# Moving the heads' norm, transposes and splits of two mixers among the units around them, on one core

## The reference, cut to what is computed

```python
def diff_attention(q, k, v, lam_vec, subln_g, lam_init):
    ...
    o = map_query_blocks(block, q)
    o = rmsnorm(o, subln_g) * (1.0 - lam_init)
    return o.reshape(B, S, A_W)
...
def odd_mixer(h, st_C, st_n, st_m, st_h, w_in, gate_b, conv_c, conv_d, conv_d_b,
              rg_wa, rg_ba, rg_wx, rg_bx, rg_lam, norm_g, w_out):
    ...
    hc = rmsnorm(hf + jnp.flip(hb, 2), norm_g)
    hc = hc.transpose(0, 2, 1, 3).reshape(B, S, C_W) * jax.nn.sigmoid(o)
    ...
    out = (jnp.concatenate([hc, hd], axis=-1) @ w_out).astype(h.dtype)
```

## Time and profile before

| | us |
|---|---|
| median of three runs | 1631.69 (1631.17 to 1632.00) |
| the profiled execution | 1632.15 |
| its span, first to last instruction | 1630.6 |
| PE, DVE, ACT busy in the span | 1477.7, 1050.4, 900.0 |
| experts, 923 to 1600 | 677.0 |

### The profile page before, as it was taken

The page is one execution under the profiler, slowest core; times in us unless marked ns, Lnnn a source line. Parts: engine busy times, 40 slices in busy tenths (PEclk is TensorE's granted clock), DMA queues, the critical chain, the costliest instruction groups (busy, mean ns, idle before and its releaser), DMA issues.

```text
span 1630.6 us, 19112 instructions
## 1 busy us (share of the span) xinstructions
PE 1477.7 (91%) x7385; PEld 1225.0 (75%) x7385; DVE 1050.4 (64%) x1270; ACT 900.0 (55%) x1062; POOL 93.2 (6%) x162
## 2 busy tenths in 40 slices
PE   4989798899999989997777899999999999999991
PEld 1987356699998878885456688888888888888881
DVE  2424546533233445894464798797987989879794
ACT  3422446533232445773155577677776877768773
POOL 0402500000000002000000200000000000000001
PEclk8999899999999999998898999999999999999996
DMA  9793990333342324224615799999999999999993
GB/s 361 206 392 119 322 338 22 103 104 104 125 134 103 129 72 161 104 80 157 238 55 207 286 351 391 371 399 374 390 389 359 408 376 392 391 367 403 379 377 129
DMA packets 146621, 414.52 MB, mean 254 GB/s; under 512 B 6924, under 2 KB 30888, under 8 KB 146408
## 3 DMA queue, kind: packets, MB, share of 16 engines
q1 hardware_dynamic: 134192, 375.93, 62.3%
q0 software_dynamic: 9600, 34.07, 5.8%
q10 hardware_dynamic: 2744, 3.36, 0.6%
HBM read 391.29 MB, written 22.95 MB: 254 GB/s over the span
## 4 chain that ended last, share of the span: by engine, by line
PE 82%; DVE 8%; DMA 4%; ACT 3%; issue 1%; POOL 1%; POOLq 0%; ACTq 0%; SPq 0%; DVEq 0%
PE bank L1852 40%; PE bank L1598 11%; PE bank L1393 6%; PE bank L1609 6%; PE bank L1442 4%; PE bank L1390 4%; PE bank L1334 2%; DMA ring<-in_w_in_even_dram 2%; PE bank L1531 2%; PE bank L1566 1%; DMA ring<-in_mod_w_dram 1%; PE bank L1820 1%; PE bank L1553 1%; PE bank L1344 1%; DMA routed<-xn,idx 1%
## 5 line engine op out<-in xcount | busy, mean ns | idle before, releaser
L1852 PE MATMUL bank<-arena_parts 128*128 128x512 f32 x1520 | 400.1, 391 | 0.9 <-DVE arena_parts L2515 0.9
L1852 PEld LDWEIGHTS bank<-arena_parts 128*128 128x128 f32 x1520 | 283.7, 188 | 62.4 <-issue 2.5
L2508 DVE TENSOR_TENSOR ring_parts<-ring,arena_parts 128x2048 fp32r<-128x2048 f32 x124 | 278.4, 2285 | 71.2 <-ACT arena_parts L1236 71.2
L1236 ACT ACTIVATE arena_parts<-ring 128x2048 fp32r<-128x2048 f32 x124 | 234.0, 1920 | 28.3 <-DMA ring<-in_moe_w_dram 26.9
L1852 PE MATMUL bank<-ring_parts,arena_parts 128*128 128x512 f32 x720 | 222.9, 391 | 0.0
L1852 PEld LDWEIGHTS bank<-ring_parts,arena_parts 128*128 128x128 f32 x720 | 135.7, 188 | 28.7
L1598 PE MATMUL bank<-ht_parts,arena_parts 128*128 128x384 f32 x352 | 118.4, 336 | 0.9 <-DVE xn_parts L1952 0.8
L1598 PE MATMUL bank<-ht_parts,ring_parts 128*128 128x384 f32 x352 | 117.6, 334 | 0.0
L1598 PE MATMUL bank<-xn_parts,arena_parts 128*128 128x384 f32 x352 | 117.6, 334 | 0.0
L1852 PE MATMUL bank<-xn_parts,arena_parts 128*128 128x512 f32 x320 | 93.5, 394 | 6.7 <-DVE ring_parts L2508 6.7
L1852 PE MATMUL bank<-ht_parts,arena_parts 128*128 128x512 f32 x320 | 94.0, 395 | 0.0
(11 more groups left out here) (423 smaller groups left out, 2688.4 us busy)
## 6 DMA issues: line engine op xcount, KB each, us to landing
ring<-in_moe_w_dram SPq DMA_DIRECT2D x184, 1024.0 KB, 7.2
arena<-in_moe_w_dram SPq DMA_DIRECT2D x60, 1024.0 KB, 6.8
ring<-in_mod_w_dram SPq DMA_DIRECT2D x24, 2048.0 KB, 8.9
ring<-in_ff_w_dram SPq DMA_DIRECT2D x23, 1024.0 KB, 7.9
ring<-in_w_in_even_dram SPq DMA_DIRECT2D x6, 2048.0 KB, 14.4
ring<-in_w_in_odd_dram SPq DMA_DIRECT2D x6, 2048.0 KB, 7.9
ring<-in_ff_w_dram SPq DMA_DIRECT2D x5, 2048.0 KB, 7.8
routed<-arena POOLq DMA_DIRECT2D x1, 7168.0 KB, 28.7
```

Of the source, the lines that this page charges most:

```text
L1236: act.activation(whi_moe[n_ % E_WHI], e_half(j, h), ACT.Copy).then_inc(whi_ready, 1)
L1852: ins = pe.matmul(bank[base + b][:, :], lhs[:, c_, :], rhs[:, k, 512 * b:512 * b + 512], start=(first and h == 0 and k == 0 and n_ == 0), ...
L2508: dve.tensor_tensor(e_half(j, h, low=True), e_half(j, h), whi_moe[(2 * j + h) % E_WHI], ALU.subtract).then_inc(wlo_ready, 1)
```

## The change

It has four parts.

1. **Attention.** The copy of a unit's product by DVE moves one iteration later, and in each iteration ahead of the work on the probabilities. The squares of the four "a" heads go into iterations 15 to 17, their sum into 19, the root into 20, the scaling into 22 to 25. Seven of eight heads are turned (PE), copied (ACT) and split (DVE) in iterations 26 to 31 and 33, all through bank 7, and four of the eight output weight quarters are split in 27, 29, 31 and 33. The two gate rows move from behind the loop into the output projection: between its two column halves of tile 0, and behind tile 0.
2. **Around the projections of "v" and "o".** DVE splits quarter 18 between two scans, 19 before the first key convolution, and joins the scans later. The logs of the first two mLSTM units move a quarter of "o" earlier. The sigmoid becomes a tanh: sigmoid(o) g = (1 + tanh(o/2)) g/2. `gate_gain` makes that, with the norm's gain in it, in units 2 to 4.
3. **The units of the mLSTM.** ACT keeps the modulation panel before the exponential of the next unit, and the "o" rows are taken before the first `inter`.
4. **Norm of the mLSTM's heads.** Heads 0 to 2 are squared and rooted by ACT in unit 6 and scaled in unit 7. Only head 3 is left for behind the last unit. The gate's multiplication is in the same instruction as the scaling. The three finished heads are turned before the last panel's transposes.

```diff
+        HEAD_AT = {26: 0, 27: 1, 28: 2, 29: 3, 30: 4, 31: 5, 33: 6}
+        OUT_AT = {27: 0, 29: 1, 31: 2, 33: 3}
...
-            act.wait_ge(o_kept, NU)
-            head_norm(0)
-            act.wait_ge(stored, 16 * 4)
-            keep_gates(0)
-            turned_heads(0)
+                if 15 <= i < 18:
+                    act.wait_ge(o_kept, 12)
+                    ins = act.activation(sq_even[:, i - 15, :, :], xnk[:, 0:4, i - 15, :], ACT.Square)
+                    if i == 17:
+                        ins.then_inc(hsq_ready, 1)
+                if i == 20:
+                    act.wait_ge(hsum_ready, 1)
+                    act.activation(hn[:, 0, 1, :], hn[:, 0, 0, :], ACT.Sqrt, scale=1.0 / P, bias=epsc[:, :])\
+                       .then_inc(hroot_ready, 1)
+                if i in HEAD_AT:
+                    keep_head(0, HEAD_AT[i])
+                if i in OUT_AT:
+                    if i == 27:
+                        act.wait_ge(stored, 16 * 4)
+                    high_out(0, OUT_AT[i])
+            high_out(0, 4)
+            keep_head(0, 7)
+            high_out(0, 5)
+            keep_gate(0, 0)
+            high_out(0, 6)
+            high_out(0, 7)
+            keep_gate(0, 1)
...
-                    act.activation(sigo[:, m, :], src[:, :], ACT.Sigmoid).then_inc(proj_act, 1)
+                    act.activation(sigo[:, m, :], src[:, :], ACT.Tanh, scale=0.5).then_inc(proj_act, 1)
...
             rg_decay(1)
+            high_quarter(1, 18)
             items_of("k", 0, 4)
-            high_quarter(1, 18)
+            high_quarter(1, 19)
             for m in range(4):
                 silu_of(m)
-            high_quarters(19, 21)
+            high_quarter(1, 20)
...
             mlstm_exp(0)
             for u, (h, d) in enumerate(munits):
                 q, r = u % 2, 32 * d + h
+                if u:
+                    keep_mod(15 + u)
                 if u + 1 < 8:
                     mlstm_exp(u + 1)
-                if u:
-                    keep_mod(15 + u)
+                if u == 6:
+                    head_squares(0, 3)
+                if u == 0:
+                    items_of("o", 0, 3)
...
+                if u == 6:
+                    head_roots(0, 3)
                 act.wait_ge(cout_kept, u + 1)
                 act.dma_start(O[6][0, 0, d, h], cout[:, q, 0:P]).then_inc(c_stored[q], 16)
                 if u == 0:
-                    items_of("o", 0, 3)
                     act.wait_ge(rg_free, 1)
...
             keep_mod(23)
-            act.wait_ge(h_ready, 8)
-            head_norm(1)
+            for k in range(3):
+                keep_head(1, k)
+            head_squares(3, 4)
+            high_out(1, 0)
+            head_roots(3, 4)
             keep_gates(2)
-            turned_heads(1)
+            high_out(1, 1)
+            keep_head(1, 3)
+            for n_ in range(2, 8):
+                high_out(1, n_)
...
+            def turn_head(m, k):
+                for t in range(NT):
+                    ins = pe.transpose(bank[head_bank(m, k)][:, P * t:P * t + P], xnk[:, k, t, :], ident)
+                ins.then_inc(o_turned, 1)
 
             def out_proj(m, t):
                 for j in range(2):
+                    if m == 0 and t == 0 and j:
+                        gate_row(0, 0)
...
+                if i in HEAD_AT:
+                    k = HEAD_AT[i]
+                    if k == 0:
+                        pe.wait_ge(mod_added, 16)
+                    else:
+                        pe.wait_ge(ot_dve, k)
+                    if k < 4:
+                        pe.wait_ge(heads_ready, k + 1)
+                    else:
+                        pe.wait_ge(o_kept, 12 + 6 * (k - 3))
+                    turn_head(0, k)
             pe.wait_ge(pts_ready, NU)
             pe.wait_ge(o_kept, NU)
-            pe.wait_ge(mod_added, 16)
-            for c_ in range(CONDS):
-                gate_row(0, c_)
-            pe.wait_ge(heads_ready, 1)
-            turn_heads(0)
-            for t in range(NT):
+            pe.wait_ge(ot_dve, 7)
+            turn_head(0, 7)
+            out_proj(0, 0)
+            gate_row(0, 1)
+            for t in range(1, NT):
                 out_proj(0, t)
...
-            project(1, 5, "o", (nothing, nothing, first_logs))
-            pe.wait_ge(sw_ready, 1)
-            mlstm_logs(1)
+            def second_logs():
+                pe.wait_ge(sw_ready, 1)
+                mlstm_logs(1)
+
+            project(1, 5, "o", (nothing, first_logs, second_logs))
...
+            pe.wait_ge(heads_ready, 5)
+            pe.wait_ge(h_ready, 7)
+            pe.wait_ge(inter_kept, 14)
+            pe.wait_ge(cout_kept, 7)
+            for k in range(3):
+                turn_head(1, k)
             mod_turn(23)
             pe.wait_ge(h_ready, 8)
             pe.wait_ge(inter_kept, 16)
             pe.wait_ge(cout_kept, 8)
             for c_ in range(CONDS):
+                pe.wait_ge(ot_dve, HEADS[1] + 2 + c_)
                 gate_row(2, c_)
+            pe.wait_ge(heads_ready, 6)
             pe.wait_ge(mod_added, 24)
-            pe.wait_ge(heads_ready, 2)
-            turn_heads(1)
+            turn_head(1, 3)
             out_proj(1, 0)
...
+                if i >= 3:
+                    u = i - 3
+                    kind, h, t, j = units[u]
+                    dve.wait_ge(pv_done, u + 1)
+                    if kind == "a":
+                        dve.tensor_copy(xnk[:, h, t, :], bank[6][:, 0:P])\
+                           .then_inc(o_kept, 1)
+                    else:
+                        dve.tensor_scalar(xnk[:, 4 + h // 2, t, HD * (h % 2):HD * (h % 2) + HD],
+                                          bank[6][:, 0:HD], rl[:, j:j + 1], None, ALU.mult)\
+                           .then_inc(o_kept, 1)
                 if turn_at(i) is not None:
                     add_mod(turn_at(i))
...
+                if i == 19:
+                    dve.wait_ge(hsq_ready, 1)
+                    dve.tensor_reduce(hn[:, 0, 0, :].rearrange("p (t h) -> p t h", t=NT), sq_even, AX.X, ALU.add)\
+                       .then_inc(hsum_ready, 1)
+                if i == 22:
+                    dve.wait_ge(hroot_ready, 1)
+                    then(dve.reciprocal(hn[:, 0, 2, :], hn[:, 0, 1, :]))
+                if 22 <= i < 26:
+                    scale_head_even(i - 22)
+                if i in HEAD_AT:
+                    low_head(0, HEAD_AT[i])
+                if i in OUT_AT:
+                    low_out(0, OUT_AT[i])
+            low_out(0, 4)
+            low_head(0, 7)
+            for n_ in range(5, 8):
+                low_out(0, n_)
...
             conv_qk(3)
             low_quarter(17, 1)
             rg_scans(1, 0)
+            low_quarter(18, 1)
             rg_scans(1, 2)
-            low_quarter(18, 1)
-            rg_join()
             low_quarter(19, 1)
             conv_qk(4)
             low_quarter(20, 1)
             conv_qk(5)
+            rg_join()
...
                     add_mod(15 + u)
+                if 2 <= u < 5:
+                    gate_gain(u - 2)
+                if u == 7:
+                    scale_heads(0, 3)
                 dve.wait_ge(inter_kept, 2 * (u + 1))
...
                     mlstm_logs(u + 2)
+                if u == 6:
+                    head_sums(0, 3)
+            for k in range(3):
+                low_head(1, k)
+            head_sums(3, 4)
+            low_out(1, 0)
+            scale_heads(3, 4)
             add_mod(23)
-            dve.wait_ge(h_ready, 8)
-            head_norm(1, sq_odd, sigo)
-            turned_heads(1)
+            low_out(1, 1)
+            low_head(1, 3)
+            for n_ in range(2, 8):
+                low_out(1, n_)
             norm_tiles(2)
```

110 lines of the change are left out of this document (44 added, 66 removed).

## The result

The changed kernel takes 1621.88 us (median of eight runs) against 1631.38 for the kernel before in the same series: ratio 0.9941, 95% interval 0.9932 to 0.9951. That is 9.5 us faster, where 23.9 were forecast, and 1.9 us above the range's end of 1620. One of the eight executions took 5169.5 us and is left out of the ratio; the median of the other seven is 1621.83. The profiled execution has a span of 1621.4 us against 1630.6.

What follows compares the result with a forecast made beforehand. PE bounds the attention loop and is busy through the experts; ACT and DVE chains bound the stretch behind attention, waits the recurrence. Even layer +5.7 and odd layer -29.6 on 1632.15, less .46, gave 1607.8 us; range 1592 to 1620.

Steps and rivals of the forecast that it cites:

- Iterations 26 to 34: Attention's last iterations: a chain through PE, ACT and DVE adds 14.4 us, a lower clock 2.5; +16.9 together.
- Rival C: Attention's last iterations: whole stretch at the lower clock, +25 to +27 instead of +16.9; 1616 to 1618 us, chance .12.
- The gate rows: Even layer's output projection: two gate rows, 16 products in all, now stand where nothing hides them; +1.8 us.
- The tail behind attention: Last attention product to first output product: norm and seven of eight heads' turns leave, 12.7 us becomes 0.7; -12.0.
- The modulation part: Attention iterations with modulation panels: squares, sum and root taken up there, DVE's copy earlier; -1.0 us, between 0 and -2.
- The start of the recurrence: Odd layer up to modulation panel 16: earlier split and logs remove PE waits; panel ends at 752.0, not 758.62; -6.6 us.
- The steps: Six recurrence steps: kept panel ahead of the exponential, 6.65 us a step instead of 9.8; -18.7 us.
- Step 7: Recurrence, kept panel 22: a new wait behind the root for heads 0 to 2 on ACT; +4.3 us.
- The odd tail: Behind the recurrence, before the output projection: only head 3's norm, turn and split remain, 9.1 us of 17.15; -8.0.
- The odd projection: Odd layer's output projection: it waits less for its weight quarters; -0.6 us.
- Rival D: Recurrence steps stay bound by DVE: division, logs and weights close a loop, 8.0 us a step; 1616 us, chance .10.
- Rival E: Recurrence: late weight panels delay the next exponential and everything; at 11.5 us a step, 1637 us; chance .03.

Runs made afterwards that it cites:

- the kernel with five edits: Changed kernel plus: head splits one iteration later, three weight quarters behind the loop, panel addition before weighing, root and squares later, odd second quarter before gate-row copies: 1592.2 us.
- the repeats over the loop's end: The kernel with five edits, with PE repeating the probabilities' transposes 3, 9 and 6 times more in attention iterations 34 to 36: 1590.7 us.

## Why the prediction was wrong

The sign held, and so did the chain named for attention's last iterations and the waits named for the start of the recurrence; the size was wrong, by 14.7 us in the span. Two terms that held in size held in part by luck.

- **Iterations 26 to 34** failed most, in one of the step's two addends. The chain was put at +14.4 and measured at +15.2 at most, with the clock kept up by repeats. The lower clock was put at 2.5 and costs 7.3 or more. I took a clock near that of the recurrence, 0.84; it was 0.57. Rival C had the right cause, and a price (+25 to +27) near the measured +22.4. I gave it .12; with a chain that leaves PE idle once in each iteration it should have had more.
- **The gate rows** were mis-sized by a reading error. `x16` at 1.78 is one gate row; I took it for two. The lists in the order of the instructions count calls, and two rows are `x16` there; the profile shows two records for each of these products, so one row is `x16` and two are `x32`. The trace of the kernel before had it, behind attention:

```profile
265.71 5.54 PE L1368 MATMUL bank<-cst,gcol 128*128 128x128 f32 x32 [0.42 <-issue]
```

  The misreading is worth 1.8 us. It also makes PE's work in the 12.7 us behind attention some 9 us, and not the 4 of the prediction. The first output products, at the lower clock behind the loop, cost 1.7 us more than at the rate of the last ones, and nothing in the sum stood for that.
- **The tail behind attention** held: -11.7 for -12.0.
- **The modulation part** did not gain 1.0 but lost 0.5. Just behind it PE waited .35 us for DVE's copy in an iteration with a scaling of heads, which I had put at nothing; the rest of the 1.5 isn't traced to a cause.
- **The start of the recurrence** held, -7.4 for -6.6. PE's waits of 4.3 and 2.0 us are gone, new ones of .7 and 1.0 stand in their place, and panel 16 takes 1.92 us instead of 3.64. No run takes these edits apart.
- **The steps** took 7.25 us each on average where 6.65 was forecast. The step that failed is that nothing was listed as late next for PE's panel products. The edit that takes the wait for the kept panel away lets PE reach the next panel earlier, and the bank was then not free, because DVE's addition stood behind the weighing, which waits for the exponential. The whole miss of 3.6 us is in the first step, 10.4 us, with the wait of 2.8 and a panel at the lower clock; that the other five came to 6.6 is luck, since each still has 1.2 to 1.3 us of that wait. The run with the addition first shows 5.9.
- **Step 7** held in size, +4.4 for +4.3, by luck in part. PE's wait grew by 2.8 us and not by 4.3; the other 1.6 are the work behind it at the lower clock, which the sum had at nothing:

```profile
816.15 0.85 PE L1373 MATMUL bank<-cst,jk 128*128 128x128 f32 x4 [3.59 <-ACT jk L936]
```

  In the kernel before, this wait was .82 ([0.82 <-ACT jk L936], at 818.00). The run that moved the root shows that it is the order on ACT that makes it.
- **The odd tail** held, -8.7 for -8.0, and this too by luck in part. The forecast followed head 3 through its norm. In the trace PE waits 1.1 us for the low parts of the other heads, which stand behind the last division on DVE, then makes the two gate rows, and turns head 3 right behind them without a wait:

```profile
824.54 3.81 PE L1397 MATMUL bank<-cst,gcol 128*128 128x128 f32 x32 [1.13 <-DVE xn_parts L2072]
828.18 0.49 PE L1451 MATMUL bank<-cst,xn 128*128 128x128 f32 x3
```

- **The odd projection** lost 1.4 instead of gaining 0.6. PE waits 1.7 us for one weight quarter that stood behind the copies of the gate rows, where it waited .4 in the kernel before. With the quarter ahead of those copies the wait is .6 (`PE bank L1469 <- DVE ring_parts L2080: 0.6, 1, 0.6`, in the kernel with five edits).

Rival D came about in kind and not in price: log weights, exponential and weighing did close a loop with PE once in each step, but through DVE's addition and the panel's bank, at 7.25 us a step and not 8.0. Rival E did not: the DMA became full only at 5.9 us a step.

## What to carry to other kernels

Work that is hung into a loop at the end of an iteration is safe only if, on every engine, it stands behind what the next iteration's first user waits for; here that was the position of DVE's two split calls, and 12 us. When a wait on a chain is removed, list what the freed engine asks for next, and whose bank that is. Price each idle gap that a change brings to TensorE twice, once for the gap and once for the clock of the work behind it; the second price is not always due, as the gaps of 1.2 us in the steps show.

## What the runs showed of the hardware

Ninety-six useless transposes made the kernel 8 us faster, because they kept the granted clock at 1.00 instead of 0.57 over 32 us. The Trainium skill ("TensorE: Matmul & The Clock Gate", "HAM oscillation — how this bites in real kernels") says that an engine that works in bursts between waits is put back to the lower level and begins each burst there. The trace of the changed kernel agrees in attention, with products of .85 us ahead of the gap of 2.64 and 1.51 behind it. It doesn't agree in the steps of the recurrence: behind five gaps of 1.16 to 1.33 us the panels take 1.92 us, as they do at full clock.

Two things no run here explains. The lower level also lasts while PE hardly waits: with the splits one iteration later PE is busy 20.04 of 21 us at 0.55. And one program can have either level. In the profiled execution with the repeats over the loop's end the clock is 1.00 up to 244 us and 0.50 from 246 on, and PE's only gap there is .35 us, ahead of 242.60; the kernel with five edits has the same gap, and its clock stays at 1.00. It costs some 12 to 13 us. An execution that much slower is seen in one of six of each of the three kernels whose heads are split one iteration later and whose quarters are behind the loop, but only this one has a trace.
